# MLA scores as three products of rounded halves, in a two-block kernel on one Trainium2 core

## Chip, core and metric
The kernel runs on one core of one Trainium2 chip. The metric is the time of one execution on the device, in microseconds (us), the lower the better. The core's engines run beside each other and wait for each other through semaphores: TensorE (matrix products, PE in the rows, its weight loads PEld), VectorE (DVE), ScalarE (ACT), GpSimd (POOL) and SyncE (SP), which here only issues the loads.

## What is computed
Two transformer blocks on 512 positions of width 1024 behind 16 meta tokens. The first is a gated recurrence and a pooling mixer with a feed-forward part; the second has two attentions side by side, MLA and Fox, with 16 heads each. The change touches only the scores of the MLA attention:

```python
k_pe = rope(k_pe_raw, pos)[:, None]
q_m = jnp.concatenate([q_nope, rope(q_pe, pos)], axis=-1)
k_m = jnp.concatenate([k_nope, jnp.broadcast_to(k_pe, (B, MLA_HEADS, L, MLA_ROPE_DIM))], axis=-1)
o_mla = causal_block_attention(q_m, k_m, v_mla, MLA_SCALE)
# inside, for each block of 128 queries:
s = jnp.einsum('bhqd,bhkd->bhqk', qb, k, preferred_element_type=jnp.float32) * scale
p = jax.nn.softmax(jnp.where(key_pos[None, :] <= qpos[:, None], s, -jnp.inf), axis=-1)
```

## The kernel before
**Products.** All large products work with operands split into two rounded halves (type fp32r): high = rounded x, low = x - high, and the product is high x high + high x low + low x high, three matmuls that accumulate in PSUM. Weights are split on the way: SyncE loads a unit of 128x2048 into `raw` (one of three slots), ScalarE rounds it into `whi` (`w_high`), VectorE writes the rest into `wlo` in place of `raw` (`w_low`). Only a few products use plain fp32 operands, among them the scores of the MLA heads (L1204); in the profile one such product is two MATMUL instructions. The Fox heads' scores (L1207, L1208) are two products of rounded operands, each of which carries halves in both parts of its 128 rows.

**The MLA loop.** `attention(A, project, ...)` exists once on each of TensorE, VectorE and ScalarE, and `gather_ends` on GpSimd. Each runs steps h = 0 to 17 in an order written out by hand. A head has four score blocks i = 0 to 3 of 128 queries by 144, 272, 400 and 528 keys (the last as two cuts of 264). PSUM banks 4, 5, 4 and 5+6 hold them, so `scores(h, i)` waits until the block two before it has been reduced (`m_ready`); `scores(h+1, 1)` thus waits for the reduce of block 3 of head h.

In step h TensorE runs: the query product mq(h+1) (six matmuls of 512 columns), scores(h,0), scores(h,1), then in odd steps from 3 on `weigh` (probabilities times values of two heads, L1248), in even steps `turn_residual` (L1233); then turn(h-1, 0..3) (transposes of the probabilities, L1221) with scores(h,2) and scores(h,3) between them, and the key product mk, one half of the next pair of heads (three matmuls of 264 columns).

VectorE (L2460 and the lines around it): `mla_project(h)`, which in odd steps scales a row block of the residual twice (hT, nzt), in even steps takes a low half (zlo), then `q_out(h+1)` (queries out of PSUM with the rope factors, L2551); reduce(h,0), reduce(h,1), at i = 1 the reciprocals, a part of the Fox gate sums and at times a `w_low` (L1897); reduce(h,2), a copy of turn 1; reduce(h,3), in odd steps the scaled output (omla, L2478), the copies of turn 3. Each reduce adds the mask, copies the block to `Pm` and takes the row extreme.

ScalarE (all through the helper at L1399): in odd steps a high half (zhi<-nzt), at times `w_high`; exp(h,0), exp(h,1); in even steps the residual's transposes (htok); the copy of turn 0; exp(h,2); `k_out`, two copies of 64x264 keys from PSUM into `kh`; exp(h,3), the copy of turn 2. exp(h,i) waits for reduce(h,i); turn(h,0) waits for exp(h,3); `weigh` waits for the copies of the turns of its two heads.

GpSimd: four small copies `Pe` (L817) behind the four exps, and four DMAs (L803) that spread a row of reciprocals.

Keys: `kh[0..3]` hold four heads, rows 0 to 63 from `k_out`, rows 64 to 127 the rope rows, which are the same for all heads and are written once (L2431, L2432, L2523, L2524). `MZ_AT` says at which steps ScalarE and VectorE (one step later) convert the weight units of the second half of the queries (uq[1]) and of the gating products (mz). `MZ_STEPS` puts the first two gating products between the last turns on TensorE.

Of the kernel before, what the change touches and what calls it, by code (L numbers as in the profile page):

```python
# [292 lines left out]
def build_program(nc: bass.Bass, a, out):  # L293
# [3 lines left out]
    with ctx:  # L297
# [128 lines left out]
        r1l, e2 = at("r1l", [P, SEQ], F32, e + 17920)  # L426
# [4 lines left out]
        PT = [at(f"PT{i}", [P, 14 * P], F32, e + i * 14 * P * 4)[0] for i in range(2)]  # L431
        Pe = [at(f"Pe{i}", [P, P], F32, e + (i + 1) * 14 * P * 4 - P * 4)[0] for i in range(2)]
# [5 lines left out]
        qh = [at(f"qh{i}", [P, SEQ], F32, e + i * SEQ * 4)[0] for i in range(2)]  # L438
# [3 lines left out]
        kh += [at(f"kh{2 + i}", [P, T], F32, e + (1 + i) * T * 4)[0] for i in range(2)]  # L442
# [81 lines left out]
        fl_abs, kr_ready = sem("fl_abs"), sem("kr_ready")  # L524
# [6 lines left out]
        class Norm:  # L531


            def __init__(self, name, src, K, n, width, sqb, ztb, rbb, gain, dst, lhs=None):
# [6 lines left out]
                if self.summed:  # L541
# [110 lines left out]
        MZ_AT = {2: (pl.uq[1],), 10: (U(("mz", 0)),), 15: (U(("mz", 2)),), 16: (U(("mz", 4)),)}  # L652
# [47 lines left out]
        def _(sp):  # L700
# [9 lines left out]
            def load(u):  # L710
# [30 lines left out]

            spill_at = 3
# [24 lines left out]
        def _(pool):  # L767
# [26 lines left out]

            def gather_ends(A):
# [11 lines left out]
                for h in range(HEADS + 2):  # L807
# [26 lines left out]
        def _(pe):  # L834
# [338 lines left out]
            pe.wait_ge(r1_log, 1)  # L1173
# [10 lines left out]
            def scores(A, h, i):  # L1184
                if 4 * h + i >= 2:
                    pe.wait_ge(A.m_ready, 4 * h + i - 1)
                if i == 0:
                    if A is mla:
                        for b in range(2):
                            tile_freed(pe, ("mk", h // 2, b))  # L1190
                        if h == 2:
                            pe.wait_ge(kr_ready, 2)
# [99 lines left out]
            pe.wait_ge(kr_ready, 1)  # L1292
# [97 lines left out]
        def _(act):  # L1390
# [293 lines left out]
            w_high(pl.uq[0])  # L1684
            tile_freed(act, ("cq", 1))
# [9 lines left out]
            A_(nrb[:, NM:T], r2t[:, :], ACT.Exp, scale=-0.5).then_inc(r2_ready, 1)  # L1695
            A_(r1[:, :], r1l[:, :], ACT.Exp, scale=-0.5).then_inc(r1_ready, 1)
# [12 lines left out]
            def k_out(x, b):  # L1709
# [4 lines left out]
                tick(A_(kh[2 * x % 4][0:NOPE, cols], acc_real(n, slice(0, NOPE), HALF), ACT.Copy))  # L1714
                tile_free(A_(kh[2 * x % 4 + 1][0:NOPE, cols], acc_real(n, slice(NOPE, P), HALF), ACT.Copy), n)
# [965 lines left out]
```

## Time and profile before

| | us |
|---|---|
| median of 3 runs (lowest, highest) | 1473.01 (1472.83, 1474.54) |
| profiled execution, its own time | 1472.77 |
| its span, first to last instruction | 1470.9 |
| TensorE busy | 1450.9 |
| VectorE busy | 834.5 |
| ScalarE busy | 691.8 |
| GpSimd busy | 115.7 |

TensorE's granted clock was 1.0 of full speed over the whole span. The MLA loop begins at about 836 us and its last scores end at about 943 us. Busy times of TensorE are modelled at their ends, since matmuls are pipelined: what one costs is read from the starts of two that follow each other.

### The profile page before, as it was taken

What the parts mean: (1) busy time and instruction counts of PE and PEld (TensorE: products, weight loads), DVE (VectorE), ACT (ScalarE), POOL (GpSimd) and SP (SyncE); (2) the same over time, 40 slices, a digit from 0 to 9 for tenths busy, and PEclk for the clock granted to TensorE, in tenths of its full rate; (3) what the DMA queues carried; (4) which work ended last, traced back from release to release, by engine and by line L of the source; (5) the groups of instructions that cost most, each with busy time, mean ns of one, the idle gap of its engine ahead of it and who ended that gap; (6) DMA issues with size and microseconds to landing.
All of it is one profiled execution on the core that took longest, in us unless ns stands there. A gap on an engine that the chain in (4) does not pass through costs nothing.

```text
span 1470.9 us, 26479 instructions
## 1 busy us (share of the span) xinstructions
PE 1450.9 (99%) x11311; PEld 1283.2 (87%) x11311; DVE 834.5 (57%) x1365; ACT 691.8 (47%) x1025; POOL 115.7 (8%) x278
## 2 busy tenths in 40 slices
PE   7999999999999999999999999999999999999998
PEld 7999999999999898998888777788899888778888
DVE  6487977764656566654335787642223566644343
ACT  6565877853443222322233676542222777743232
POOL 0000000000000000000000044300000233320000
PEclk9999999999999999999999999999999999999999
DMA  7222121124322223222334333433223333342222
GB/s 245 87 75 80 60 87 59 59 73 143 131 88 87 86 90 112 87 86 85 103 101 108 63 48 20 77 97 105 86 86 90 67 71 71 72 106 92 86 94 80
DMA packets 138969, 130.25 MB, mean 89 GB/s; under 512 B 26569, under 2 KB 134884, under 8 KB 138596
## 3 DMA queue, kind: packets, MB, share of 16 engines
q1 hardware_dynamic: 134084, 120.39, 26.0%
q0 software_dynamic: 4752, 8.16, 5.3%
q8 instruction: 90, 1.47, 0.4%
q14 instruction: 27, 0.22, 0.0%
q10 hardware_dynamic: 16, 0.00, 0.0%
HBM read 119.69 MB, written 4.26 MB: 84 GB/s over the span
## 4 chain that ended last, share of the span: by engine, by line
PE 91%; DVE 4%; ACT 3%; issue 1%; DMA 0%; SPq 0%; DVEq 0%; ACTq 0%
PE PS L922 79%; PE PS L1248 3%; PE PS L1221 2%; PE PS L1204 2%; DVE wlo L1897 1%; PE PS L1208 1%; PE PS L1207 1%; ACT L1399 1%; PE PS L1033 1%; ACT whi L1399 0%; DMA xt<-in_x 0%; ACT Pm L1399 0%; PE PS L989 0%; PE PS L1089 0%; DVE zlo L1945 0%
## 5 line engine op out<-in xcount | busy, mean ns | idle before, releaser
L922 PE MATMUL PS<-zhi,whi 128*128 128x258 f32 (+2 forms) x1856 | 486.9, 320 | 3.1 <-ACT hT L1399 1.4
L922 PE MATMUL PS<-zhi,wlo 128*128 128x258 f32 (+2 forms) x1856 | 476.8, 314 | 0.0
L922 PE MATMUL PS<-zlo,whi 128*128 128x258 f32 (+2 forms) x1856 | 475.4, 314 | 0.6 <-DVE zlo L1945 0.6
L922 PEld LDWEIGHTS PS<-zhi,whi 128*128 128x128 f32 x1856 | 306.9, 189 | 27.9 <-issue 1.9
L922 PEld LDWEIGHTS PS<-zhi,wlo 128*128 128x128 f32 x1856 | 305.6, 189 | 22.3
L922 PEld LDWEIGHTS PS<-zlo,whi 128*128 128x128 f32 x1856 | 305.5, 189 | 20.8 <-DVE zlo L1945 0.9
L1897 DVE TENSOR_TENSOR wlo<-raw,whi 128x2048 fp32r<-128x2048 f32 (+2 forms) x114 | 247.8, 2174 | 124.7 <-ACT whi L1399 124.6
L1399 ACT ACTIVATE whi<-raw 128x2048 fp32r<-128x2048 f32 (+2 forms) x114 | 207.5, 1820 | 152.7 <-DMA raw<-in_w_up 57.0
L1399 ACT ACTIVATE Pm<-Pm,small 128x144 f32<-128x144 f32 (+3 forms) x128 | 73.1, 572 | 38.5 <-DVE small L2460 38.2
L2460 DVE CUSTOM_DVE_ANT_0 Pm<-PS,cmask 128x144 f32<-128x144 f32 (+3 forms) x128 | 62.9, 504 | 35.8 <-PE PS L1204 21.5
L922 PE MATMUL PS<-glo,whi 128*128 128x512 f32 x176 | 69.9, 397 | 0.0
L922 PE MATMUL PS<-ghi,whi 128*128 128x512 f32 x176 | 69.7, 396 | 0.0
L922 PE MATMUL PS<-ghi,wlo 128*128 128x512 f32 x176 | 69.1, 392 | 0.0
L1399 ACT ACTIVATE nsq<-PS 128x512 f32<-128x512 f32 x32 | 19.0, 595 | 99.5 <-PE PS L922 92.1
L1221 PE MATMUL PS<-ident,Pm 128*128 128x128 f32 x320 | 53.8, 274 | 1.6 <-ACT PT L1399 1.0
L817 POOL COPY Pe<-Pm 128x16 f32<-128x16 f32 x128 | 43.0, 349 | 149.0 <-ACT Pm L1399 148.9
L1221 PEld LDWEIGHTS PS<-ident,Pm 128*128 128x128 f32 x320 | 39.9, 140 | 14.2 <-ACT PT L1399 3.4
L1399 ACT ACT_TABLE_LOAD x37 | 47.5, 1283 | 7.8 <-PE PS L922 7.1
L922 PE MATMUL PS<-yhi,whi 128*128 128x512 f32 x128 | 51.1, 399 | 0.0
L922 PE MATMUL PS<-yhi,wlo 128*128 128x512 f32 x128 | 50.4, 394 | 0.0
L922 PE MATMUL PS<-ylo,whi 128*128 128x512 f32 x128 | 50.2, 392 | 0.0
L1399 ACT ACTIVATE E<-E 128x1056 f32<-128x1056 f32 (+2 forms) x32 | 33.6, 1049 | 31.8 <-DVE E L2044 26.8
(357 smaller groups left out, 2132.9 us busy)
## 6 DMA issues: line engine op xcount, KB each, us to landing
raw<-in_w_in SPq DMA_DIRECT2D x50, 1024.0 KB, 5.3
raw<-in_w_up SPq DMA_DIRECT2D x22, 1024.0 KB, 5.1
raw<-in_w_out SPq DMA_DIRECT2D x8, 1024.0 KB, 5.2
raw<-in_w_down SPq DMA_DIRECT2D x8, 1024.0 KB, 5.1
raw<-in_w_br_mla SPq DMA_DIRECT2D x4, 1024.0 KB, 5.3
raw<-in_w_br_fox SPq DMA_DIRECT2D x4, 1024.0 KB, 5.1
raw<-in_w_down SPq DMA_DIRECT2D x4, 768.0 KB, 4.4
hspill<-hT SPq DMA_DIRECT2D x1, 2112.0 KB, 7.6
```

The lines of the kernel that those rows point to most:

```text
L817: nc.gpsimd.tensor_copy(Pe[h % 2][:, 32 * i:32 * i + NM], Pm[h % 2][:, o_:o_ + NM])\
L922: ins = mm(o_, l_, r_, start=first, stop=last)
L1033: ins = mm(dst.rearrange("p (n b) -> p n b", b=half), e[:, hh, t0 + r:t0 + r + 32], rhs, start=True, stop=True)
L1204: ins = mm(dst, qh[h % 2][:, t0:t0 + P], kh[h % 4][:, c0:c1], start=True, stop=True)
L1207: mm(dst, xqa[i_][:, t0:t0 + P], xka[i_][:, c0:c1], start=True, stop=False)
L1208: ins = mm(dst, xqb[i_][:, t0:t0 + P], xkb[i_][:, c0:c1], start=False, stop=True)
L1221: ins = tr(PS[:, 2 + g % 2, P * x:P * (x + 1)], Pm[h % 2][:, o_:o_ + P], ident[:, :])
L1248: mm(PS[64 * r:64 * r + 64, 7, P * j:SEQ], vtok[:, j, v0:v0 + DV], PT[r][:, G_COL[j]:G_COL[j] + G_N[j]], start=j == 0, stop=False, skip_gr ...
L1399: return nc.scalar.activation(out_, in_, func, **kw)
L1897: V.tensor_tensor(lo[s_][:, 0:n_], raw[s_][:, 0:n_], hi[s_][:, 0:n_].bitcast(F32), ALU.subtract)\
L2460: V.tensor_tensor_reduce(out=cut(Pm[h % 2][:, ATT_OFF[i]:ATT_OFF[i] + ATT_N[i]]), in0=s_view(i), in1=cut(cmask[:, T - ATT_N[i]:T]), op0=AL ...
```

## The change
- The four `kh` tiles become `khi` (type fp32r), and low halves `klo` are added for each head. They lie in weight slots that are idle at that time (`klo_a` beside the unit of w_ukv, `klo_b` in uq[0]'s slot, `klo_c` in uq[1]'s), the queries' sum `qsum` and low half `qlo` too.
- `scores` issues three matmuls a cut in place of one fp32 product.
- ScalarE: `k_out` writes the rounded high half; new is `q_high(h+1)` in step h at i = 1, between htok and the copy of turn 0.
- VectorE: `q_out` writes `qsum`; new is `k_low`, two subtractions of 64x264 that read PSUM, at i = 3 ahead of reduce(h,3). It frees the PSUM tile in place of `k_out`.
- GpSimd: new is `query_low(h+1)` in step h ahead of the copy at i = 2, and `rope_rows` in steps 0, 3 and 11.
- The rope rows of heads 0 and 1 are summed once; ScalarE rounds them, VectorE writes their low halves. TensorE waits for these (`K_LOW`) before mq(0).
- Since the low halves lie in weight slots, the loads of uq[1], mz(0) and mz(2) wait for the scores of 4, 12 and 16 heads, and their conversions move to later steps (`MZ_AT`).
- Six semaphores of one chain become `roots_step`; PT, Pe and r1l move in memory.

```diff
-        kh = [at(f"kh{i}", [P, T], F32, e + i * T * 4)[0] for i in range(2)]
+        khi = [at(f"khi{i}", [P, T], F32R, e + i * T * 4)[0] for i in range(2)]
...
+        qsum = [at(f"qsum{i}", [P, SEQ], F32, hi_of(pl.ukv) + 4 * D + i * SEQ * 4)[0] for i in range(2)]
+        qlo = [at(f"qlo{i}", [P, SEQ], F32R, hi_of(pl.ukv) + 4 * D + i * SEQ * 4)[0] for i in range(2)]
...
+        klo = [*klo_a, *klo_c, *klo_a, *klo_b, *klo_a, *klo_b, *klo_a, *klo_c]
+        K_SUM, K_HIGH, K_LOW, K_SECOND, K_FOURTH, K_LAST = 1, 3, 5, 9, 11, 13
...
-        MZ_AT = {2: (pl.uq[1],), 10: (U(("mz", 0)),), 15: (U(("mz", 2)),), 16: (U(("mz", 4)),)}
+        MZ_AT = {5: (pl.uq[1],), 13: (U(("mz", 0)),), 16: (U(("mz", 2)),), 17: (U(("mz", 4)),)}
...
+                if u in SCORES_READ:
+                    sp.wait_ge(mla.s_done, 4 * SCORES_READ[u])
...
+            SCORES_READ = {pl.uq[1]: 4, U(("mz", 0)): 12, U(("mz", 2)): HEADS}
...
+            def rope_rows(h):
+
+                done = {0: K_LOW, 3: K_SECOND, 11: K_FOURTH}[h]
+                pool.wait_ge(mla.e_ready, 4 * h + 3)
+                pool.wait_ge(q_lo, h + 2)
...
+                for n, (dst, src) in enumerate(pairs):
+                    nc.gpsimd.tensor_copy(dst[64:P, :], src[64:P, :]).then_inc(kr_step, 1)
+                    pool.wait_ge(kr_step, done + n + 1)
+
+            def query_low(x):
+
+                pool.wait_ge(q_hi, x + 1)
+                nc.gpsimd.tensor_tensor(qlo[x % 2][:, :], qsum[x % 2][:, :], qhi[x % 2][:, :].bitcast(F32), ALU.subtract)\
+                  .then_inc(q_lo, 1)
...
                     for i in range(QB):
+                        if A is mla and i == 2 and h + 1 < HEADS:
+                            query_low(h + 1)
+                        if A is mla and i == 3 and h in (0, 3, 11):
+                            rope_rows(h)
                         pool.wait_ge(A.p_exp, 4 * h + i + 1)
...
+                        pe.wait_ge(q_lo, h + 1)
...
+                if A is mla:
+                    for x, (lhs, rhs) in enumerate(((qhi[h % 2], khi[h % 4]), (qhi[h % 2], klo[h]), (qlo[h % 2], khi[h % 4]))):
+                        for dst, c0 in cuts:
+                            c1 = c0 + dst.shape[-1]
+                            ins = mm(dst, lhs[:, t0:t0 + P], rhs[:, c0:c1], start=x == 0, stop=x == 2)
...
-            pe.wait_ge(kr_ready, 1)
+            pe.wait_ge(kr_step, K_LOW)
...
+            act.wait_ge(kr_step, K_SUM)
+            for i in range(2):
+                A_(khi[i][64:P, :], PT[0][64:P, 0:T], ACT.Copy).then_inc(kr_step, 1)
...
-                tick(A_(kh[2 * x % 4][0:NOPE, cols], acc_real(n, slice(0, NOPE), HALF), ACT.Copy))
-                tile_free(A_(kh[2 * x % 4 + 1][0:NOPE, cols], acc_real(n, slice(NOPE, P), HALF), ACT.Copy), n)
+                for r in range(2):
+                    A_(khi[2 * x % 4 + r][0:NOPE, cols], acc_real(n, slice(NOPE * r, NOPE * (r + 1)), HALF), ACT.Copy)\
+                        .then_inc(k_hi, 1)
+
+            def q_high(x):
+                tile_freed(act, ("mq", x))
+                A_(qhi[x % 2][:, :], qsum[x % 2][:, :], ACT.Copy).then_inc(q_hi, 1)
...
-            attention(mla, mla_project, lambda h: None, mla_after)
+            attention(mla, mla_project, lambda h: q_high(h + 1) if h < HEADS - 1 else None, mla_after)
...
-            tick(V.tensor_tensor(kh[0][r_, :], t1, t2, ALU.add))
-            V.tensor_tensor(kh[1][r_, :], t1, t2, ALU.add).then_inc(kr_ready, 1)
+            V.tensor_tensor(t1, t1, t2, ALU.add).then_inc(kr_step, 1)
...
+            dve.wait_ge(kr_step, K_HIGH)
+            V.tensor_tensor(klo_a[1][r_, :], t1, khi[1][r_, :].bitcast(F32), ALU.subtract).then_inc(kr_step, 1)
             v_out(2, 1)
             norm_lo(normq, 0)
             norm_lo(normq, 1)
             v_out(3, 1)
             v_out(4, 1)
+            V.tensor_tensor(klo_a[0][r_, :], t1, khi[0][r_, :].bitcast(F32), ALU.subtract).then_inc(kr_step, 1)
...
+            def attention(A, project, between, ahead, after):
                 for h in range(HEADS + 2):
                     project(h)
                     for i in range(4):
+                        if i == 3:
+                            after(h)
                         if h < HEADS:
                             dve.wait_ge(A.s_done, 4 * h + i + 1)
...
+            def k_low(x, b):
+                n, cols = ("mk", x, b), slice(HALF * b, HALF * (b + 1))
+                dve.wait_ge(k_hi, 4 * x + 2 * b + 2)
...
+                for r in range(2):
+                    ins = V.tensor_tensor(klo[2 * x + r][0:NOPE, cols], acc_real(n, slice(NOPE * r, NOPE * (r + 1)), HALF),
+                                          khi[2 * x % 4 + r][0:NOPE, cols].bitcast(F32), ALU.subtract)
...
+            def mla_after(h):
+                if h < HEADS - 2:
+                    k_low(h // 2 + 1, h % 2)
...
+            w_low(*MZ_AT[HEADS + 1])
```

## Rows read from the trace of the kernel before

**Rows 1.** Page, busy us (share of the span) xinstructions.
```profile
PE 1450.9 (99%) x11311; PEld 1283.2 (87%) x11311; DVE 834.5 (57%) x1365; ACT 691.8 (47%) x1025; POOL 115.7 (8%) x278
```
**Rows 2.** Timeline of TensorE in step 7: start us, us, engine, line, operation.
```profile
881.85 2.37 PE L1248 MATMUL PS<-PT,vtok 128*64 128x512 f32 x16
...
885.17 0.84 PE L1204 MATMUL PS<-kh,qh 128*128 128x400 f32 x2
885.84 0.49 PE L1221 MATMUL PS<-ident,Pm 128*128 128x128 f32 x3
```
**Rows 3.** Timeline of TensorE and its weight loads in a Fox step.
```profile
1191.90 0.19 PEld L1208 LDWEIGHTS PS<-xkb,xqb 128*128 128x128 f32 x1
1192.01 0.19 PEld L1207 LDWEIGHTS PS<-xka,xqa 128*128 128x128 f32 x1
...
1197.68 0.34 PE L1208 MATMUL PS<-xkb,xqb 128*128 128x400 f32 x1
1197.87 0.39 PE L922 MATMUL PS<-zhi,whi 128*128 128x512 f32 x1
```
**Rows 4.** Timeline of VectorE: reduces of heads 0, 6, 7, 8 and 13.
```profile
839.87 0.71 DVE L2460 CUSTOM_DVE_ANT_0 Pm<-PS,cmask 128x528 f32<-128x528 f32 x1 [0.67 <-PE PS L1204]
...
879.41 0.71 DVE L2460 CUSTOM_DVE_ANT_0 Pm<-PS,cmask 128x528 f32<-128x528 f32 x1 [0.34 <-PE PS L1204]
...
887.26 0.71 DVE L2460 CUSTOM_DVE_ANT_0 Pm<-PS,cmask 128x528 f32<-128x528 f32 x1 [0.17 <-PE PS L1204]
...
890.44 0.44 DVE L2460 CUSTOM_DVE_ANT_0 Pm<-PS,cmask 128x272 f32<-128x272 f32 x1
...
893.15 0.71 DVE L2460 CUSTOM_DVE_ANT_0 Pm<-PS,cmask 128x528 f32<-128x528 f32 x1 [0.33 <-PE PS L1204]
...
928.56 0.71 DVE L2460 CUSTOM_DVE_ANT_0 Pm<-PS,cmask 128x528 f32<-128x528 f32 x1
```
**Rows 5.** Timeline of ScalarE in steps 7 and 8.
```profile
881.01 0.38 ACT L1399 ACTIVATE PT<-PS 128x256 f32<-128x256 f32 x1
...
886.66 0.63 ACT L1399 ACTIVATE Pm<-Pm,small 128x400 f32<-128x400 f32 x1 [0.69 <-DVE small L2460]
...
887.28 0.78 ACT L1399 ACTIVATE kh<-PS 64x264 f32<-64x264 f32 x2
...
891.49 0.58 ACT L1399 ACTIVATE htok<-PS 128x512 f32<-128x512 f32 x1
891.96 0.58 ACT L1399 ACTIVATE PT<-PS 128x512 f32<-128x512 f32 x1
892.44 0.62 ACT L1399 ACTIVATE Pm<-Pm,small 128x400 f32<-128x400 f32 x1
...
893.05 0.79 ACT L1399 ACTIVATE kh<-PS 64x264 f32<-64x264 f32 x2
```
**Rows 6.** Groups of ScalarE from 836 to 943 us: xcount, busy us, mean ns, idle.
```profile
L1399 ACT ACTIVATE whi<-raw 128x2048 fp32r<-128x2048 f32 x3 | 5.7, 1906 | 0.0
...
L1399 ACT ACTIVATE zhi<-nzt 128x512 fp32r<-128x512 f32 x8 | 5.0, 630 | 4.8 <-DVE nzt L2534 4.8
```
**Rows 7.** Groups of VectorE from 812 to 943 us.
```profile
L2431 DVE TENSOR_TENSOR kh<-PT 64x528 f32<-64x528 f32 x1 | 0.7, 706 | 0.0
```
**Rows 8.** Timeline ahead of the MLA loop, VectorE and TensorE.
```profile
832.61 1.40 DVE L2419 COPY vtok<-PS 128x512 f32<-128x512 f32 x2
...
836.57 1.67 PE L1204 MATMUL PS<-kh,qh 128*128 128x144 f32 x5
```
**Rows 9.** Timeline of VectorE and GpSimd in step 3.
```profile
856.21 2.27 DVE L1897 TENSOR_TENSOR wlo<-raw,whi 128x2048 fp32r<-128x2048 f32 x1
...
856.22 2.46 POOL L817 COPY Pe<-Pm 128x16 f32<-128x16 f32 x2
```
**Rows 10.** Groups of GpSimd over the whole span.
```profile
L773 POOL TENSOR_SCALAR_AFFINE_SELECT ident<-ident 128x128 f32<-128x128 f32 x1 | 0.3, 284 | 0.2 <-POOL ones L771 0.2
```
**Rows 11.** Page, DMA issues: xcount, KB each, us to landing.
```profile
raw<-in_w_in SPq DMA_DIRECT2D x50, 1024.0 KB, 5.3
```

More of the change, by code:

```diff
@@ L430, in build_program @@
         e += 2 * 1344 * 4
-        PT = [at(f"PT{i}", [P, 14 * P], F32, e + i * 14 * P * 4)[0] for i in range(2)]
-        Pe = [at(f"Pe{i}", [P, P], F32, e + (i + 1) * 14 * P * 4 - P * 4)[0] for i in range(2)]
+        PT = [at(f"PT{i}", [P, 1344], F32, e + i * 1344 * 4)[0] for i in range(2)]
+        Pe = [at(f"Pe{i}", [P, P], F32, e + (26 + i) * P * 4)[0] for i in range(2)]
         e += 2 * 14 * P * 4
@@ L523, in build_program @@
         ht_turned, ht_copied = sem("ht_turned"), sem("ht_copied")
-        fl_abs, kr_ready = sem("fl_abs"), sem("kr_ready")
+        fl_abs, kr_step = sem("fl_abs"), sem("kr_step")
+        q_hi, q_lo, k_hi = sem("q_hi"), sem("q_lo"), sem("k_hi")
         fox_hi, fox_lo = sem("fox_hi"), sem("fox_lo")
@@ L793, in move_ends @@
                     nc.gpsimd.dma_start(vtok[32 * i:32 * i + NM, QB, :], vtok[0:NM, i + 1, :]).then_inc(A.v_moved, 16)
+            def rope_rows(h):
+                done = {0: K_LOW, 3: K_SECOND, 11: K_FOURTH}[h]
+                pool.wait_ge(mla.e_ready, 4 * h + 3)
+                pool.wait_ge(q_lo, h + 2)
+                pairs = [(dst, klo_a[1]) for dst in (klo_b if h == 3 else klo_c)]
+                if h == 0:
+                    pool.wait_ge(kr_step, K_LOW)
+                    pairs = [(khi[2], khi[0]), (khi[3], khi[0])] + pairs
+                else:
+                    tile_done(pool, ("mq", h + 1))
+                for n, (dst, src) in enumerate(pairs):
[5 more added lines that the diff above has]
+                  .then_inc(q_lo, 1)
             def gather_ends(A):
@@ L825, in _ @@
             pool.wait_ge(e_cleared, 2)
+            query_low(0)
             gather_ends(mla)
@@ L1190, in scores @@
                             tile_freed(pe, ("mk", h // 2, b))
+                        pe.wait_ge(q_lo, h + 1)
                         if h == 2:
[L1192 removed]
+                            pe.wait_ge(kr_step, K_SECOND)
+                        elif h == 6:
+                            pe.wait_ge(kr_step, K_FOURTH)
+                        elif h == 14:
+                            pe.wait_ge(kr_step, K_LAST)
                     else:
@@ L1748, in mla_project @@
                     k_out(0, 1)
+                    q_high(0)
                 if h == 1:
@@ L2448, in _ @@
             v_out(4, 1)
-            def attention(A, project, between, ahead):
+            V.tensor_tensor(klo_a[0][r_, :], t1, khi[0][r_, :].bitcast(F32), ALU.subtract).then_inc(kr_step, 1)
+            def attention(A, project, between, ahead, after):
                 for h in range(HEADS + 2):
@@ L2522, in mla_project @@
                     q_out(0)
-                    tick(V.tensor_copy(kh[2][r_, :], kh[0][r_, :]))
-                    V.tensor_copy(kh[3][r_, :], kh[1][r_, :]).then_inc(kr_ready, 1)
+                    k_low(0, 0)
+                    k_low(0, 1)
                     q_out(1)
                 if h == 1:
-                    dve.wait_ge(r1_ready, 1)
-                    dve.wait_ge(r2_ready, 1)
+                    dve.wait_ge(roots_step, R1_READY)
                 if h % 2 == 1 and h < HEADS:
@@ L2558, in mla_ahead @@
                     w_low(*MZ_AT.get(h - 1, ()))
-            attention(mla, mla_project, lambda h: None, mla_ahead)
+            attention(mla, mla_project, lambda h: None, mla_ahead, mla_after)
+            w_low(*MZ_AT[HEADS + 1])
             def gated(kind, A, b):
@@ L2637, in _ @@
             attention(fox, fox_project, lambda h: split_lo(h + 1) if h < HEADS - 1 else None,
-                      lambda h: w_low(*XU_AT.get(h, ())))
+                      lambda h: w_low(*XU_AT.get(h, ())), lambda h: None)
             gated("xz", fox, 1)
```

53 lines of the change are left out of this document (31 added, 22 removed).

## Prediction

> **What bounds the kernel now.** I read the busy totals first: TensorE is busy 99% of the span, no other engine over 57% [rows 1]. So nothing is gained except by giving TensorE less to do, and anything that makes TensorE wait is paid in full. Only the attention of the MLA heads changes, so I then read one pair of its steps on TensorE, VectorE and ScalarE. The ruler is the reduce of the last score block, reduce(h,3), on VectorE: heads 6, 7 and 8 start it at 879.41, 887.26 and 893.15 [rows 4]. A step that ends with an odd head (it holds a weigh) takes 7.85 us, one that ends with an even head 5.89. TensorE is back to back through both, so today TensorE sets the pace, and the chains between the engines have some slack. The question is how much slack the new links use.
>
> **What the change saves.** A plain fp32 score block of 400 columns takes 885.84 - 885.17 = 0.67 us [rows 2], that is 1.67 ns a column, or 2.25 us for the 1344 columns of a head. The Fox heads show what one product of rounded operands costs: 400 columns from 1197.68 to 1197.87, 0.18 us (0.46 ns a column) [rows 3]. A short product is limited by its weight load: 144 columns take 0.11, the distance between two loads (1191.90, 1192.01) [rows 3]. Three products then cost 3 x 0.11 for block 0, 3 x 0.13 for 272 columns, 3 x 0.18 for 400 and 6 x 0.12 for 2 x 264: 1.98 us. TensorE saves 0.27 us a head, 4.4 us over 16 heads. That is all the change can win, 0.3% of the span, and only where TensorE stays the bound.
>
> **What it adds to the chain.** T is the start of reduce(h-1,3). TensorE may not start scores(h,1) before reduce(h-1,3) is done, because both use bank 5. The change puts two new links in front of reduce(h,3), both in order on their engines: ScalarE's q_high(h+1), which stands ahead of the copy of turn 0, exp(h,2) and the two key copies; and VectorE's k_low, which waits for those key copies and stands ahead of reduce(h,3) itself. So reduce(h,3), which today only waits for TensorE, will wait for exp(h,2) and all that ScalarE does behind it.
>
> Prices: q_high is a rounding copy of 128x512 on ScalarE; the same shape (zhi) shows 0.63 [rows 6], 0.10 of it under the next instruction, so 0.53 (bounds 0.45 to 0.63). k_low is two VectorE operations of 64x264; the nearest row is the 128x272 reduce, 0.44, of which 0.36 until the next can start [rows 4]; I take 0.35 each, 0.70 for the pair (bounds 0.5 to 0.9).
>
> *Even head (step 8, T = 887.26).* VectorE works back to back from T (reduce, omla, three small copies, zlo, q_out, two reduces); reduce(8,1) starts at 890.44 [rows 4], and exp(8,1) has left ScalarE at 891.49 [rows 5], T + 4.23. Then htok (0.47), the new q_high (0.53), the copy of turn 0 (0.48) and exp(8,2) (0.61) [rows 5] give T + 6.32; the key copies take 0.79 [rows 5]: T + 7.11; 0.06 to wake VectorE and 0.70 for k_low: reduce(8,3) starts at T + 7.87. Today it is T + 5.89. TensorE needs about 5.6, so the chain decides.
>
> *Odd head (step 7, T = 879.41).* The weigh needs the copy of turn 2 of head 5, which follows exp(6,3): it starts at 881.01 and takes 0.38 [rows 5], so the weigh starts at T + 2.0 at the earliest (today 881.85, T + 2.44, behind TensorE's own work [rows 2]). From the weigh to the key copies a chain runs through keys, turn 0, scores(7,2), reduce, exp(7,2) (886.66) to 887.28 [rows 2, 5]: 5.43, less 0.12 for the cheaper block: 5.31, T + 7.31. Key copies 0.78, waking 0.06, k_low 0.70: T + 8.85. Today T + 7.85. q_high lies in ScalarE's wait for turn 0 and costs nothing here.
>
> Thirteen reduces follow that of head 0: 7 odd at 8.85 and 6 even at 7.87 are 109.2 us. Off this: head 1 has no weigh but three gate operations on ScalarE instead, and head 2 has no omla; I take 1.3 for both. On top: the weight steps now lie on the chain. In step 6 w_low (2.27 [rows 9]) stands between reduce(6,1) and reduce(6,2): about 1.5; in steps 5 and 13 w_high (1.91 [rows 6]) stands ahead of exp(h,0): 0.4 each. Together 110.2. Today the same stretch is 928.56 - 839.87 = 88.7 [rows 4], its weight steps included. **The steps cost 21.5 us more.**
>
> **The start.** TensorE now waits before mq(0) for K_LOW, the low rope rows of head 0, which VectorE writes behind its last v_out. Today that ends at 832.61 + 1.40 = 834.0 [rows 8]; one more 64x528 subtraction ahead of it (0.62 of the 0.71 of such a row [rows 7]) and the last one itself bring 835.2. Then mq(0), six products of 512 columns at 0.46 ns, 1.4; four key copies 1.6; q_high 0.63; and the first query_low on GpSimd. That last one, a two-input 128x512 operation on GpSimd, has no row. Its bounds are 0.69 (VectorE's time for that shape, near the 0.71 of [rows 7]) and 2.46 (two tiny copies held up [rows 9]); the nearest is a GpSimd operation over 128 columns, 0.28 [rows 10], four times which is 1.1, and I take that. With some waking, scores(0,0) starts at 840.5 instead of 836.57 [rows 8]: 3.9. In step 0, q_high, the key copies and k_low ahead of reduce(0,3) add 1.4. **Start: 5.3.**
>
> The GPSIMD Engine Reference of the Trainium skill (section 3.1, side-by-side cycle accounting) gives about 2.6 cycles an element for a two-input operation, at 1.2 GHz: an estimate of 1.1 us for 512 columns, which would leave the sum as it is; no row of this case shows the operation.
>
> **The end.** In step 14 w_low of mz0 stands before reduce(14,2), and scores(15,0), (15,1) and the weigh of step 15 follow late: 1.6. Behind it TensorE is the bound again and has 0.3 less to do in head 15. The later weights: mz2 may load only when all scores are read; load, w_high and w_low take 5.3 + 1.9 + 2.3 = 9.5 us [rows 6, 9, 11], and between the last scores and mz2 TensorE has 13 of the 16 steps of mz0 and mz1 (13 x 3 x 0.235 = 9.2 us), eleven turns and a weigh of 2.4, so they fit; mz4 wants its w_low before the first gating product, which delays that by 2.3, still ahead of the slots that TensorE waits for. SP's loads queue behind these waits in order, and none comes too late since the steps are slower. **End: 1.3.**
>
> **Costed at nothing.** query_low within the steps: q_high is done at T + 5.3 and TensorE asks for q_lo only shortly before T + 8.6 (even), so the cover holds up to 2.9 us. The rope rows copied by GpSimd (steps 0, 3, 11) have two steps of time each. Merged semaphores and moved buffers change no order. ScalarE's two copies of rope rows lie in its idle time between w_high(uq0) and the next square. On VectorE one 64x528 sum goes, and so do two copies in step 0; neither was awaited.
>
> **Sum.** 21.5 + 5.3 + 1.3 = 28.1 on 1472.77, the profiled execution's own time (span 1470.9; the median of the runs, 1473.01, is 0.2 higher and makes no difference): 1500.9 us. Going through the bounds: k_low 0.5 to 0.9 is -2.6 to +2.6, q_high 0.45 to 0.63 in the even steps and the start -0.6 to +0.7, the first query_low -0.4 to +1.4, my reading of weight steps and waking +-2.5: together 22 to 35, or 1495 to 1508.
>
> **Rivals.**
> (A) *The slack is larger than I read and TensorE stays the bound:* then it is the start, 3.9, less 4.4, about 1472.3. For it: TensorE is at 99%, VectorE and ScalarE are under 60%. Against: k_low waits in order ahead of reduce(h,3), and scores(h+1,1) needs that reduce. It would decide only if the chain were shorter than TensorE's 5.6 and 7.6, that is over 2.2 us less in even steps. 8%.
> (B) *Only the even steps stretch,* since the weigh of the odd step and the chain behind it overlap more than I think: 7 x 7.55 + 6 x 7.87 + 1.0 = 101.1, that is 12.4 + 6.6 = 19: about 1492. 9%.
> (C) *GpSimd becomes the bound:* query_low takes over 2.9 us and q_lo decides. For it: at 856.22 two copies of 16 columns took 2.46 us together, while VectorE ran a w_low with two SBUF inputs from 856.21 for 2.27 us [rows 9], so one engine can hold the other up. Each us over 2.9 costs 6 us in the even steps and, from 4.2, 7 in the odd; at 4.3 us it is 9, with 3 more at the start: about 1513. 8%. SBUF — State Buffer, a page of the Trainium skill (section SBUF: two separate sides), says that a VectorE operation with two SBUF inputs and a GpSimd operation that reads SBUF exclude each other for a whole instruction; the trace agrees, and by that rule query_low, which falls in VectorE's wait for the key copies, would be held up only in steps 6 and 14.
> (D) *Three products take no less time than the fp32 product* (short ones limited by loads): nothing changes but 1 to 4 us, since TensorE isn't the bound; it lies in my range.
> My own sum: 72%; 3% is for what I haven't thought of.
>
> **How the numbers follow.** The predicted time is the sum, 1501. The bounds give 1495 to 1508; to leave out no more than 2 in 10 the range reaches down to B, 1490, and up to 1510. About 0.2%, 3 us, is what a measurement can tell from no change; faster by more than that needs A and a start that costs little: 0.03. Within it: the rest of A, 0.06. Slower: 0.91.
>
> **What would show it.** Right: reduce(h,3) at distances of 7.9 and 8.9 instead of 5.9 and 7.85; TensorE idle about 1 us at a time before scores(h+1,1), released by VectorE; k_low released by ScalarE's key copies; the stretch from reduce(0,3) to reduce(13,3) about 110 us; the granted clock of TensorE still 1.0. Wrong: TensorE busy throughout at steps of 5.6 and 7.6 (A), waits of TensorE on GpSimd's qlo (C), or odd steps still at 7.6 (B).

## The result, and the profile after

The changed kernel takes 1506.4 us (median of 4 runs, 1505.5 to 1510.0), the kernel before beside it 1473.8 (4 runs, 1472.8 to 1474.6): **ratio 1.0226, interval 1.0214 to 1.0238, slower**. Forecast were 1501.0 us and a range of 1490 to 1510. The profiled execution of the changed kernel took 1505.5 us, its span is 1503.7, 32.8 more than before.

The page of the changed kernel, busy us with the share of the span, and under it the chain that ended last by engine. It answers [rows 1]:

```profile
PE 1459.4 (97%) x11391; PEld 1291.1 (86%) x11391; DVE 848.4 (56%) x1396; ACT 701.5 (47%) x1043; POOL 141.4 (9%) x302
...
PE 84%; DVE 7%; ACT 5%; issue 3%; DMA 0%; SPq 0%; POOL 0%; DVEq 0%; ACTq 0%; POOLq 0%
```

The page hardly shows the loss: TensorE is still at 97%. The loss is all in the MLA loop, and there a table by stretch shows it. Each row below is the stretch from reduce(0,3) to reduce(13,3); the columns are its length, the busy time (and number of instructions) of TensorE, its weight loads, VectorE, ScalarE and GpSimd, the granted clock of TensorE, and the DMA share and rate in GB/s. First the kernel before, then the changed one:

```profile
839.90:928.60 88.70, 87.84 (x533) 66.05 (x531) 71.75 (x215) 64.50 (x173) 39.69 (x100) 1.00 0.36 31
```
```profile
847.70:960.20 112.50, 93.99 (x596) 71.48 (x596) 80.86 (x239) 71.67 (x186) 59.58 (x120) 1.00 0.34 34
```

Before, TensorE is busy 87.8 of 88.7 us: it sets the pace. After, it is idle for 18.5 of 112.5 us. No engine fills the stretch any more; a chain through several of them sets it, as the rows below and the experiments show.

VectorE's timeline of the changed kernel, the reduces of heads 0, 7, 8, 9, 13 and 15 and the k_low pairs ahead of two of them, answers [rows 4]:

```profile
847.72 0.71 DVE L2521 CUSTOM_DVE_ANT_0 Pm<-PS,cmask 128x528 f32<-128x528 f32 x1
...
908.44 0.71 DVE L2521 CUSTOM_DVE_ANT_0 Pm<-PS,cmask 128x528 f32<-128x528 f32 x1
...
915.57 0.89 DVE L2620 TENSOR_TENSOR klob<-PS,khi 64x264 fp32r<-64x264 f32 x2 [1.60 <-ACT khi L1444]
916.49 0.71 DVE L2521 CUSTOM_DVE_ANT_0 Pm<-PS,cmask 128x528 f32<-128x528 f32 x1
...
924.67 0.89 DVE L2620 TENSOR_TENSOR klob<-PS,khi 64x264 fp32r<-64x264 f32 x2 [1.00 <-ACT khi L1444]
925.59 0.71 DVE L2521 CUSTOM_DVE_ANT_0 Pm<-PS,cmask 128x528 f32<-128x528 f32 x1
...
960.24 0.71 DVE L2521 CUSTOM_DVE_ANT_0 Pm<-PS,cmask 128x528 f32<-128x528 f32 x1
...
975.74 0.71 DVE L2521 CUSTOM_DVE_ANT_0 Pm<-PS,cmask 128x528 f32<-128x528 f32 x1 [0.17 <-PE PS L1247]
```

The even step (head 7 to 8) takes 8.05 us and the odd one (8 to 9) 9.10, where 5.89 and 7.85 stood. VectorE sits idle for 1.60 and 1.00 us until ScalarE's key copies release k_low, and the reduce comes right behind the pair. What k_low waits for is in ScalarE's timeline of step 8 (answers [rows 5]): htok, q_high, the copy of turn 0, exp(8,2), key copies, back to back:

```profile
912.66 0.57 ACT L1444 ACTIVATE htok<-PS 128x512 f32<-128x512 f32 x1
...
913.14 0.62 ACT L1444 ACTIVATE qhi<-qsum 128x512 fp32r<-128x512 f32 x1
...
913.66 0.58 ACT L1444 ACTIVATE PT<-PS 128x512 f32<-128x512 f32 x1
...
914.14 0.62 ACT L1444 ACTIVATE Pm<-Pm,small 128x400 f32<-128x400 f32 x1
...
914.75 0.79 ACT L1444 ACTIVATE khi<-PS 64x264 fp32r<-64x264 f32 x2
```

TensorE's timeline shows the other end of the chain, scores(9,1) behind the reduce and the weigh behind ScalarE's copy:

```profile
917.26 0.39 PE L1247 MATMUL PS<-khi,qhi 128*128 128x272 f32 x1 [0.62 <-DVE small L2521]
...
918.53 0.65 PE L1293 MATMUL PS<-PT,vtok 128*64 128x512 f32 x2 [0.63 <-ACT PT L1444]
```

The 32.8 us by place: reduce(0,3) comes at 847.72 instead of 839.87, 7.85 late; reduce(0,3) to reduce(13,3) takes 112.52 instead of 88.69, 23.83 more; from there to reduce(15,3) 15.50 instead of 14.58 (928.56 to 943.14), 0.92 more. From reduce(15,3) to the end of the span both take 528 us, the changed kernel 0.2 more.

### The profile page after: what moved, and what is told of

The parts are those of the page before. It is cut to its first block, busy times and chain, and to the rows that moved or that the text cites. A ratio compares the mean times of both kernels' runs of the same rounds, so it can differ in the third digit from the quotient of the medians.

```text
span 1503.7 us, 26747 instructions
## 1 busy us (share of the span) xinstructions
PE 1459.4 (97%) x11391; PEld 1291.1 (86%) x11391; DVE 848.4 (56%) x1396; ACT 701.5 (47%) x1043; POOL 141.4 (9%) x302
## 4 chain that ended last, share of the span: by engine, by line
PE 84%; DVE 7%; ACT 5%; issue 3%; DMA 0%; SPq 0%; POOL 0%; DVEq 0%; ACTq 0%; POOLq 0%
PE PS L959 76%; PE PS L1293 2%; PE PS L1266 1%; ACT Pm L1444 1%; DVE wlo L1954 1%; DVE Pm L2521 1%; ACT khi L1444 1%; PE PS L1253 1%; PE PS L1252 1%; ACT whi L1444 1%; ACT L1444 1%; PE PS L1070 1%; DMA xt<-in_x 0%; ACT PT L1444 0%; PE PS L1026 0%
## 5 line engine op out<-in xcount | busy, mean ns | idle before, releaser
L959 PEld LDWEIGHTS PS<-zhi,wlo 128*128 128x128 f32 x1856 | 305.6, 189 | 22.3
L1266 PEld LDWEIGHTS PS<-ident,Pm 128*128 128x128 f32 x320 | 39.1, 140 | 18.5 <-ACT PT L1444 6.5
```

The lines of the kernel that those rows point to most:

```text
L959: ins = mm(o_, l_, r_, start=first, stop=last)
L1266: ins = tr(PS[:, 2 + g % 2, P * x:P * (x + 1)], Pm[h % 2][:, o_:o_ + P], ident[:, :])
```

## Experiments

Each is an edit of the changed kernel, except one of the kernel before; the diffs are shortened to what they do. Distances between the fourth reduces, in us, each to about 0.01, read from VectorE's timeline of the profiled execution (first: where reduce(0,3) starts; even: head 7 to 8; odd: head 8 to 9; step 6: head 5 to 6; 0 to 13 and 13 to 15: heads):

| kernel | first | even | odd | step 6 | 0 to 13 | 13 to 15 | median us |
|---|---|---|---|---|---|---|---|
| before | 839.87 | 5.89 | 7.85 | 5.89 | 88.69 | 14.58 | 1473.8 |
| changed | 847.72 | 8.05 | 9.10 | 9.31 | 112.52 | 15.50 | 1506.4 |
| k_low behind the reduce | 847.71 | 6.89 | 8.32 | 9.50 | 100.14 | 18.97 | 1495.5 |
| two products | 848.16 | 8.06 | 8.92 | 9.30 | 111.76 | 17.17 | 1507.6 |
| wait for rope rows late | 844.49 | 8.05 | 9.09 | 9.30 | 112.46 | 15.55 | 1502.8 |
| without k_low | 845.47 | 5.64 | 8.09 | 7.30 | 90.19 | 15.50 | 1481.6 |
| without low queries | 847.79 | 7.53 | 9.09 | 9.30 | 109.17 | 17.21 | 1502.4 |
| neither low half | 844.19 | 5.60 | 7.62 | 7.35 | 87.47 | 15.52 | 1477.0 |
| k_low on the same rows | 848.04 | 7.79 | 8.85 | 9.05 | 109.57 | 15.50 | 1502.8 |
| neither, and wait late | 841.48 | 5.64 | 7.64 | 7.35 | 87.52 | 15.51 | 1474.1 |
| four moves together | 845.13 | 6.29 | 8.10 | 8.90 | 95.48 | 18.82 | 1486.4 |
| before, weight split moved | 840.24 | 5.90 | 7.85 | 7.29 | 89.91 | 14.57 | 1474.4 |

The kernel before took 1473.7 to 1474.4 beside each of them.

The column "first" also holds what happened far ahead of the change. Against the changed kernel (835.81) mq(0) starts 2.1 us later in the profiled execution with k_low behind the reduce, 1.8 with two products, 2.1 without low queries and 0.8 on the same rows; with four moves it starts at 835.90, 2.8 later than in the run with the late wait alone (833.13). In each of these five the granted clock of TensorE had fallen below 1.0 in one to three windows of 10 us ahead of 210 us (0.66 to 0.95 there). The edits don't touch what runs there, so this has to be taken off "first" in them.

**k_low behind the reduce.**
```diff
-                        if i == 3:
-                            after(h)              # k_low
                         ... reduce(h, i)
+                        if i == 3:
+                            after(h)
```


> Changed kernel with one move: VectorE subtracts the low half of the keys behind the step's fourth maximum (reduce 3) and not ahead of it. Theory of the chain (the end of a step is exp 2, khi x2, k_low x2, reduce 3, and k_low delays reduce 3): reduce 3 of each step starts some 0.9 us earlier against exp 2, most of that is kept in odd steps (no more than 1.5 us, since PE's own work of about 7.6 us bounds them) and less in even ones, where the later k_low is in front of the next step's first VectorE work; even steps about 7.4, odd about 7.6, time about 1493 us. Rival (steps set by something else, e.g. by PE's products or GpSimd): steps stay at 8.06 and 9.1 to 9.3, time 1505 to 1507 us.

1495.5 us (1493.3 to 1496.6), ratio 1.014, interval 1.0125 to 1.0155. The pair of steps is 15.2 us long where 15.0 was expected; the even step gained more (to 6.89) and the odd one less (8.32). VectorE's timeline of this kernel, reduce(8,3), the k_low pair and reduce(9,3):

```profile
909.00 0.71 DVE L2519 CUSTOM_DVE_ANT_0 Pm<-PS,cmask 128x528 f32<-128x528 f32 x1
...
910.53 0.89 DVE L2620 TENSOR_TENSOR klob<-PS,khi 64x264 fp32r<-64x264 f32 x2 [0.82 <-ACT khi L1444]
...
917.32 0.71 DVE L2519 CUSTOM_DVE_ANT_0 Pm<-PS,cmask 128x528 f32<-128x528 f32 x1
```

The reduce no longer waits for the key copies. So the order k_low before reduce, and with it the wait for ScalarE, is worth 12.4 us of stretch (112.52 to 100.14), and about 2 us more in step 0: mq(0) started 2.1 us late and reduce(0,3) did not. Behind head 13 this kernel takes 3.5 us more than the changed one: 2.2 in step 14 (8.97 for 6.77), where w_low stands, and 1.3 in step 15 (10.00 for 8.73), where the granted clock had fallen (0.67 from 956.8 to 960 us).

**The third product left out, and k_low left out.** If TensorE set the steps, leaving out the third product would bring the most; if the chain does, leaving out k_low.
```diff
-enumerate(((qhi, khi), (qhi, klo), (qlo, khi)))
+enumerate(((qhi, khi), (qhi, klo)))               # two products
```
```diff
-enumerate(((qhi, khi), (qhi, klo), (qlo, khi)))
+enumerate(((qhi, khi), (qhi, khi), (qlo, khi)))   # without k_low
-k_low(0, 0); k_low(0, 1); after(h): k_low(h // 2 + 1, h % 2)
```


> Changed kernel with the third product of the scores (low queries by high keys) left out, all waits kept; the scores are less exact. Takes about 0.66 us of TensorE's work out of each of 16 heads. Theory of the chain (VectorE and ScalarE set the steps): only what of it lies on the chain goes, some 0.2 us a head or less, time 1502 to 1505 us. Rival (TensorE sets the steps): the whole 0.66 x 16 = 10.6 us goes, time about 1496 us.

> Changed kernel without the low half of the keys' first 64 rows: VectorE's k_low pairs are left out, the second product reads the high half in their place (scores wrong by that), ScalarE's copy frees the tile. Theory of the chain: with k_low gone reduce 3 needs only scores 3 and the step is bounded by TensorE again; even steps 5.9 to 6.4 (5.89 before, plus what of q_high's 0.53 is on the chain), odd about 7.7; the start loses about 1.8 us of its 7.85. Time about 1483 us. Rival (q_high, query_low or the three products carry the loss): steps stay above 7.5 and 8.7, time above 1498 us.

Taking about 0.66 us a head from TensorE (a third of the forecast 1.98) moves the stretch by 0.8 us and brings nothing in the time (1507.6, 1506.3 to 1509.7). Part of that is the clock: in the profiled execution 1.8 us were lost ahead of mq(0) and 1.7 behind head 13, and the granted clock was below 1.0 in parts of the stretch. But where it was 1.0, from 912 to 960 us, an even step still takes 8.05 (925.46 to 933.51) and an odd one 8.92 (916.54 to 925.46), 0.18 less than in the changed kernel; so the 0.66 does not come back at the full clock either. Taking k_low away moves it by 22.3 us, to 1481.6 (1480.7 to 1483.3), ratio 1.0049. TensorE isn't the bound, the chain through k_low is. The timelines without k_low: VectorE's reduces of heads 7, 8 and 9; then ScalarE's q_high and copy of turn 0 and TensorE's next turn at the end of step 8; then ScalarE's q_high and copy of turn 0 in step 9:

```profile
894.37 0.71 DVE L2520 CUSTOM_DVE_ANT_0 Pm<-PS,cmask 128x528 f32<-128x528 f32 x1
...
900.01 0.71 DVE L2520 CUSTOM_DVE_ANT_0 Pm<-PS,cmask 128x528 f32<-128x528 f32 x1
...
908.10 0.71 DVE L2520 CUSTOM_DVE_ANT_0 Pm<-PS,cmask 128x528 f32<-128x528 f32 x1
```
```profile
899.12 0.62 ACT L1444 ACTIVATE qhi<-qsum 128x512 fp32r<-128x512 f32 x1
899.64 0.58 ACT L1444 ACTIVATE PT<-PS 128x512 f32<-128x512 f32 x1
```
```profile
900.27 0.55 PE L1266 MATMUL PS<-ident,Pm 128*128 128x128 f32 x3 [0.30 <-ACT PT L1444]
```
```profile
904.81 0.61 ACT L1444 ACTIVATE qhi<-qsum 128x512 fp32r<-128x512 f32 x1
906.49 0.60 ACT L1444 ACTIVATE PT<-PS 128x512 f32<-128x512 f32 x1 [1.06 <-PE PS L1266]
```

The even step falls below that of before (5.64 for 5.89), the odd one stays at 8.09, 0.24 over it.

**Without the low half of the queries, and with neither low half.**
```diff
-q_out: qsum; q_high(h + 1); query_low(h + 1)
+q_out writes qhi; third product (qhi, khi)        # without low queries
```


> Changed kernel without the low half of the queries: VectorE writes the rounded query directly, ScalarE's q_high and GpSimd's query_low are left out, the third product reads the high half (scores less exact). Theory of the chain: even steps lose q_high's 0.53 us (it stands between exp 1 and the PT copy), odd steps none or little, the first head's scores start some 1.9 us earlier; sum about 7 x 0.53 + 1.9 = 5.6 us, time about 1501 us. Rival (query_low on GpSimd bounds the steps): odd and even steps fall to below 7 and 8, time below 1490 us.

> Changed kernel with neither low half: no k_low, no q_high, no query_low; the three products read high halves only (scores less exact and wrong by that), the rope rows of the keys stay as they are. Theory (both low halves carry the whole loss of the steps, the three products themselves cost no more than the old one): steps as before or shorter (even 5.6 to 5.9, odd 7.6 to 7.9), the start keeps the 2.8 us stall of TensorE, time 1472 to 1477 us. Rival (the loads of the weights moved to other steps, the copies of rope rows or the products have a cost of their own): time above 1479 us.

Without the low queries the time is 1502.4 us (1501.0 to 1503.8), 4.0 less and not 5.6. The steps did as expected: even 8.05 to 7.53, which is q_high's 0.52, odd unchanged. Counted from mq(0) the start did too: to the first scores it is 4.96 us instead of 6.91 (837.92 to 842.88, 835.81 to 842.72). But mq(0) itself came 2.1 us later in this profiled execution, and the stretch from head 13 to 15 is 1.7 us longer than in the changed kernel, behind a clock that had fallen (0.69 from 965 to 968 us). With neither low half the time is 1477.0 (1476.4 to 1478.7), at the upper end of what was expected, and the even step lies 0.29 and the odd one 0.23 under that of before: that is the saving of TensorE. The odd distance shows one thing more: 8.09 with q_high and 7.62 without. By the rows above this half microsecond is not that of the q_high in the odd step, behind which ScalarE sits idle for 1.06 us. It is that of the even step before: q_high (899.12) pushes the copy of turn 0 to 899.64, and TensorE, which needs that copy for its next turn, starts it at 900.27, 1.28 us behind the start of the even head's last scores group (898.99) where 0.81 stands with neither low half (896.49 to 897.30). That lies behind reduce(8,3), so the ruler counts it to the odd head. With k_low in place the 0.52 shows in the even distance instead, since reduce(8,3) itself waits for what follows q_high on ScalarE. The run with neither low half lacks query_low too, but without k_low TensorE waited for query_low only once, 1.4 us at the start.

**The k_low pair.** Its two subtractions start 0.46 us apart and the reduce another 0.46 behind, though each shows about 0.43. The second reads PSUM rows 64 to 127, the first and the reduce start at row 0.
```diff
-acc_real(n, slice(NOPE * r, NOPE * (r + 1)), HALF)
+acc_real(n, slice(0, NOPE), HALF)                 # both read rows 0 to 63
```


> Changed kernel in which the second of the two k_low subtractions reads PSUM rows 0 to 63 like the first and not rows 64 to 127 (the low half of the odd heads' keys wrong by that). Theory (the second subtraction is held until the first has ended, 0.46 us behind it, because they start at different rows): distance falls to about 0.35, each step is 0.1 us shorter, time about 1504.5 us. Rival (0.46 us is the plain distance of two such operations): distance and steps stay, time 1506 us.

VectorE's timeline of this kernel, the pair of step 8 and reduce(8,3):

```profile
914.43 0.77 DVE L2620 TENSOR_TENSOR klob<-PS,khi 64x264 fp32r<-64x264 f32 x2 [1.59 <-ACT khi L1444]
915.12 0.69 DVE L2521 CUSTOM_DVE_ANT_0 Pm<-PS,cmask 128x528 f32<-128x528 f32 x1
```

The pair takes 0.69 us until the reduce starts, against 0.92, and every step is about 0.25 shorter (8.05 to 7.79, 9.10 to 8.85): both distances had been stretched, that between the two and that to the reduce. 1502.8 us (1502.4 to 1505.0), 3.6 less, where 1.5 to 2 was expected with only one of the two in mind. The Trainium skill's page VectorE: DVE Perf Modes (section Two Vector instructions with no wait between them) states this as a model: an instruction is held until all earlier ones have finished when its input starts in another group of 32 partitions than the last one read from the same memory. Both distances of the changed kernel (0.46 and 0.46), and both of this one (0.35 and 0.34), agree with it.

**The start.** TensorE's timeline of the changed kernel: the first product of mq(0) behind its wait, the first of mk, and the first of the scores; then the granted clock by stretch (last columns: clock, DMA share, GB/s):

```profile
835.81 0.50 PE L959 MATMUL PS<-cqhi,whi 128*128 128x512 f32 x1 [2.42 <-DVE kloa L2507]
...
838.12 0.42 PE L959 MATMUL PS<-ckhi,whi 128*128 128x264 f32 x1
...
842.72 0.31 PE L1247 MATMUL PS<-khi,qhi 128*128 128x144 f32 x1 [1.57 <-POOL qlo L824]
```
```profile
835.80:838.10 2.30, 2.29 (x6) 1.80 (x7) 0.00 (x0) 0.00 (x0) 0.59 (x2) 0.62 0.71 86
838.10:839.40 1.30, 1.30 (x7) 1.27 (x6) 0.69 (x1) 0.38 (x1) 0.00 (x0) 0.50 0.00 0
```

Behind the idle 2.42 us the clock fell to half, the lower level of 1.2 GHz, and mq(0) took 2.31 us (835.81 to 838.12) where the forecast had 1.4 for the six products. The first query_low (of the group of 16 below, GpSimd from 836 to 980 us) was the next wait:

```profile
L824 POOL TENSOR_TENSOR qlo<-qsum,qhi 128x512 fp32r<-128x512 f32 x16 | 20.4, 1274 | 10.5 <-ACT qhi L1444 10.5
```

```diff
-pe.wait_ge(kr_step, K_LOW)        # ahead of mq(0)
 ... scores(0, 0):
+pe.wait_ge(kr_step, K_LOW)
```


> Changed kernel with one wait moved: TensorE waits for the low rope rows of the keys (K_LOW) in front of the first scores and not in front of the first query product, which doesn't read them. Theory (the stall of 2.8 us between the last values' product and mq(0), and the half clock behind it in the changed kernel's profile, 2.3 us for mq(0) in place of 1.5, lie on the path of the start): the stall shrinks to under 0.6 us and mq(0) takes 1.5 us or less, the first scores come 2.4 to 3.9 us earlier, time about 1503 us. Rival (something else, such as VectorE's q_out or the vtok copies, is just as late): the first scores move by under 0.5 us and the time stays at 1506 us.

TensorE's timeline of that kernel, the same first and last products:

```profile
833.13 0.47 PE L959 MATMUL PS<-cqhi,whi 128*128 128x512 f32 x1
...
839.49 0.31 PE L1249 MATMUL PS<-khi,qhi 128*128 128x144 f32 x1 [1.34 <-POOL qlo L824]
```

No stall, full clock in mq(0), the first scores 3.23 us earlier and 1502.8 us (1502.1 to 1503.8), 3.6 less. The steps are untouched.

**The best case.** With neither low half and with the late wait the loop has little of the change left but the cheaper products, the copies of rope rows on GpSimd and the moved weight splits.

> The kernel with neither low half (no k_low, q_high, query_low; scores less exact and wrong by that) and with TensorE's wait for the rope rows in front of the first scores: what the change would come to if both low halves were hidden entirely. Theory: 1477.0 less the 3.3 to 3.6 us that the moved wait gave alone, 1473.4 to 1473.8 us, no more than a tie with the kernel before, since what the cheaper products save is given back by the weight splits moved to step 6 and behind step 13. Rival (the cheaper products can win once nothing else stands in the way): 1471 us or less.

1474.1 us (11 runs, 1473.8 to 1476.7), ratio 1.0005, interval 0.9996 to 1.0014: a tie, 0.3 above the 1473.8 expected at most. So even if the operations for both low halves were hidden, the change as it places the weight splits would not pay. Its windows and VectorE's timeline of step 6 (reduce(5,3), w_low, reduce(6,3)) say why:

```profile
841.50:929.00 87.50, 84.68 (x597) 70.93 (x595) 69.67 (x214) 63.98 (x174) 43.38 (x108) 1.00 0.43 43
```
```profile
874.06 0.71 DVE L2519 CUSTOM_DVE_ANT_0 Pm<-PS,cmask 128x528 f32<-128x528 f32 x1
...
878.31 2.22 DVE L1952 TENSOR_TENSOR wlo<-raw,whi 128x2048 fp32r<-128x2048 f32 x1
...
881.41 0.69 DVE L2519 CUSTOM_DVE_ANT_0 Pm<-PS,cmask 128x528 f32<-128x528 f32 x1
```

TensorE is busy 3.2 us less in the stretch (84.7 for 87.8), but the stretch is only 1.2 shorter: step 6 takes 7.35 us with w_low in it, where an even step takes 5.64; the start is 1.6 late and the end takes 0.9 more. The 1.6 of the start were not taken apart.

**The moved split alone**, in the kernel before:
```diff
-MZ_AT = {2: (pl.uq[1],), ...
+MZ_AT = {5: (pl.uq[1],), ...
```


> Kernel before with one part of the change alone: the split of the second query weight unit is moved from steps 2 and 3 (ScalarE, VectorE) to steps 5 and 6. Theory: step 5 to 6 of the trace grows from 5.89 to about 7.3 us (w_low's 2.27 us stand in front of reduce 2 there), and one of steps 1 to 3 shrinks by less than 0.6 us; time about 1474.8 us, 1.0 to 1.5 us over before. Rival (the split costs the same at either place): time within 0.3 us of before.

In the trace step 6 grows to 7.29 (873.49 to 880.78) and step 7 by 0.2, step 3 shrinks by 0.41: 1.2 us in all. The timed runs say 1474.4 beside 1474.2, ratio 1.0006, interval 0.9997 to 1.0015. The mechanism is shown in the trace; its price in the time is too small to be settled.

**Four moves together**, which leave nothing out: k_low behind the reduce, the late wait, zlo of the even steps given to GpSimd in the odd ones, q_high of even steps ahead of exp(h,0).

> Changed kernel, exact as it is, with four moves: k_low behind reduce 3; TensorE's wait for the rope rows in front of the first scores; the low half of the normed input (zlo, 0.68 us on VectorE in every even step) given to GpSimd in the odd steps; ScalarE's q_high of even steps ahead of exp 0. Theory (VectorE bounds the even steps once k_low is off the chain: in the run with k_low behind reduce 3 its work fills 6.6 of 6.9 us): even steps 6.1 to 6.4, odd 8.0 to 8.3, start 3 us earlier, time 1483 to 1488 us. Rival (ScalarE's exp and khi chain bounds them): even steps stay at 6.9, time 1491 to 1493 us.

1486.4 us (1485.7 to 1489.0), ratio 1.0084, interval 1.0067 to 1.0101: 20 us of the 32.6 are recovered. The timelines of VectorE (reduce(7,3), reduce(8,3)), of GpSimd and of ScalarE show the two works in their new places:

```profile
897.32 0.71 DVE L2529 CUSTOM_DVE_ANT_0 Pm<-PS,cmask 128x528 f32<-128x528 f32 x1
...
903.61 0.71 DVE L2529 CUSTOM_DVE_ANT_0 Pm<-PS,cmask 128x528 f32<-128x528 f32 x1
```
```profile
897.81 1.29 POOL L829 TENSOR_TENSOR zlo<-nzt,zhi 128x512 fp32r<-128x512 f32 x1
```
```profile
901.09 0.63 ACT L1452 ACTIVATE qhi<-qsum 128x512 fp32r<-128x512 f32 x1 [1.68 <-DVE qsum L2618]
```

Even steps are at 6.29. VectorE's work did bound them at 6.89 with k_low behind the reduce alone: there VectorE was back to back from 902.11 to 909.00 but for the wait in the row below, and zlo, which held it for 0.60 (905.16 to 905.76), is just what the step has lost. q_high was moved in the same run; what that move is worth by itself was not tried.

```profile
903.10 0.89 DVE L2620 TENSOR_TENSOR kloa<-PS,khi 64x264 fp32r<-64x264 f32 x2 [0.28 <-ACT khi L1444]
```

Behind head 13 the kernel with four moves loses 3.3 us against the changed one (18.82 for 15.50): 1.6 in step 14 (8.35 for 6.77) and 1.7 in step 15 (10.47 for 8.73). In step 14 w_low holds up VectorE's copy of turn 1 and TensorE behind it, which is busy 2.73 of 4.0 us; behind that the clock falls, and the weigh of step 15 takes 4.07 us where 2.37 stood in [rows 2]. The windows, and TensorE's row of that weigh:

```profile
945.00:949.00 4.00, 2.73 (x18) 2.00 (x16) 4.00 (x11) 2.88 (x8) 3.95 (x7) 1.00 0.54 35
949.00:952.00 3.00, 2.53 (x12) 1.46 (x14) 2.96 (x11) 1.75 (x6) 1.84 (x5) 0.82 0.08 8
952.00:956.00 4.00, 4.00 (x22) 2.13 (x19) 0.33 (x3) 1.22 (x5) 1.53 (x5) 0.71 0.61 35
```
```profile
950.85 4.07 PE L1302 MATMUL PS<-PT,vtok 128*64 128x512 f32 x16 [0.26 <-ACT PT L1452]
```

The best case only ties, so no arrangement of the low halves that keeps these places for the weight splits can be expected to beat the kernel before. Other places for the splits, or for the low halves in memory, were not tried.

## Why the prediction was right, point by point

- **What bounds.** Right: TensorE before, the chain after. The waits of TensorE from 830 to 980 us in the changed kernel (engine, line, what it waited for: us, times, longest) show it:

```profile
PE PS L1247 <- DVE small L2521: 9.5, 14, 1.4
...
PE PS L1293 <- ACT PT L1444: 4.0, 7, 0.6
PE PS L1266 <- ACT PT L1444: 3.3, 9, 0.6
...
PE PS L1247 <- POOL qlo L824: 1.6, 1, 1.6
```
- **What the products save.** Forecast 0.27 us a head. With neither low half the steps are 0.29 and 0.23 under those of before: right. (Sixteen times 0.27 is 4.3, not 4.4.)
- **q_high.** Forecast 0.53 in even steps, nothing in odd; measured 0.52 and 0.01. Right, and it holds without k_low too: the q_high of the odd step stands in ScalarE's wait for turn 0 there as well.
- **k_low.** The place was right, the size was off: 0.92 us until the reduce starts, not 0.70. I had priced it by a reduce with the same start row as its neighbours; on the same rows it is 0.69. This is the term that was mis-sized: 13 x 0.22 = 2.9 us. The bound of 0.9 just missed it.
- **Even and odd step.** With 0.92 for the pair the forecast chains give 7.87 + 0.22 = 8.09 and 8.85 + 0.22 = 9.07; measured 8.05 and 9.10. The chains were read rightly from [rows 4] and [rows 5].
- **Stretch.** 110.2 forecast, 113.1 with the corrected pair, 112.5 measured. Step 6 is 9.31, 1.26 over an even step, for which 1.5 stood. Steps 5 and 13 are 0.22 over an odd step each, for which 0.4 stood. That is most of the 0.6 by which 113.1 is too much.
- **Start.** 5.3 forecast, 7.85 measured. This term was too small by 2.5. Three of its links were later or longer than priced: mq(0) starts at 835.81 for 835.2, it takes 2.31 for 1.4 at the fallen clock, and query_low takes 1.26 for 1.1. And one link had no term in my sum: the keys' first product, three matmuls of 264 columns, stands between mq(0) and the key copies, and from its start to that of ScalarE it took 0.90 at the half clock (838.12 to 839.02; in the kernel before, at full clock, 0.65, 834.15 to 834.80). The key copies took 1.52 for 1.6 until q_high, and the waking less than I had allowed. The GPSIMD Engine Reference of the Trainium skill (section 3.1) gives about 2.6 cycles an element for such an operation, from which 1.1 is an estimate; the rows show 1.27 in the mean of 16, and they decide. In step 0 the rest is 1.7 (7.85 less the 6.15 by which the first scores are late) for 1.4. My line "the granted clock still 1.0" failed here, and nowhere else in the loop of this profiled execution.
- **End.** 1.3 forecast, 0.92 measured, and 528 us from reduce(15,3) to the end in both: the weights moved behind the loop cost nothing, as worked out.
- **Rivals.** A (slack) falls by the reduce's distances and by the run without the third product. B (only even steps) falls: odd steps grew by 1.25. C (GpSimd) falls: TensorE waited for qlo once, 1.6 us at the start, and query_low took 1.27, not 2.9. In steps 6 and 14 query_low did start only behind VectorE's w_low (at 896.61 and 966.28; w_low ends at 896.46 and 966.13), as forecast under C, and TensorE did not wait for it. D (products no cheaper) falls by the steps with neither low half.

The sum was 28.1 and the span grew by 32.8: 2.3 of the gap is k_low in the stretch (net of step 6 and small terms), 2.6 the start, and the end gave 0.4 back. The range did not hold by errors that cancel: all but the last point the same way, and the mechanism is the one forecast.

## What to carry to other kernels

An operation that is put in order ahead of the link that frees a PSUM bank costs more than itself, since it makes that link wait for whatever feeds the operation: here 0.92 us of work cost 2.4 us in each even step (8.05 with it, 5.64 without) and 1.0 in each odd one, and moving it behind the link gave back a third of the whole loss. Before splitting a product that is slow on the busiest engine, compare what it saves there (here some 4.3 us) with a run in which the new side work is left out altogether: the best case was a tie. When pricing back-to-back VectorE operations, look at which partition each input starts at.

## What the runs showed of the hardware

- Two VectorE operations of 64x264 start 0.46 us apart when their PSUM inputs start at rows 0 and 64, and 0.35 apart when both start at row 0; the 128-row operation behind follows at 0.46 and 0.34.
- A stall of TensorE can be followed by a fall of its clock, but isn't always. Before mq(0) the wait for the rope rows made the same gap of 2.8 us between starts in seven profiled executions. In five of them (the changed kernel, k_low behind the reduce, without k_low, neither low half, k_low on the same rows) mq(0) then took 1.8 to 2.3 us, in two (two products, without low queries) 1.5. Behind the waits of steps 14 and 15 the clock fell in the runs with k_low behind the reduce, with two products, without low queries and with the four moves, whose last stretch is 1.7 to 3.5 us longer, in part by it, and stayed at 1.0 in the others. The same four, and that with k_low on the same rows, also show a clock below 1.0 ahead of 210 us, where the kernels don't differ. What decides it is not settled by these runs.
- The kernel with two products did less on TensorE and was no faster; from 848 to 960 us the granted clock was 0.95 where the changed kernel had 1.00.
